# First mixer: the rotation's powers computed directly behind the angles

## The reference

```python
h = rmsnorm(x); z = h @ w_in                      # (tokens, 1536): u of group A, u and v of group B
dt = exp(log_dt); mag = exp(lam_re * dt)
ab = mag * (cos(lam_im * dt) + 1j * sin(lam_im * dt))
bb = (ab - 1) / lam * B                           # B: 32 groups x 64 states x 16 inputs
h[t] = ab * h[t-1] + bb @ u[t]                    # complex, one state vector per group
yA = glu(gelu(Re(C h) + D * u))
yB = gelu(uB) * (tril(W_s) @ layernorm(gelu(vB)) + b)
x = x + [rmsnorm(yA), rmsnorm(yB)] @ w_out
x = x + FFN(rmsnorm(x))                           # layer 0: dense SwiGLU, layer 1: top-2-of-8 experts
```

## Time and profile before

| | us |
|---|---|
| median of three executions | 865.59 |
| the profiled execution | 866.52 |
| its span, first to last instruction | 864.7 |
| PE busy | 820.4 (95%) |
| DVE busy | 564.0 (65%) |
| ACT busy | 403.0 (47%) |
| POOL busy | 243.9 (28%) |

### The profile page before, as it was taken

How to read it: one execution, slowest core, us unless ns; L and a number is a source line. 1 busy time by engine, 2 the same in 40 slices (tenths; PEclk the granted TensorE clock), 3 DMA queues, 4 the chain that set the end, 5 groups by cost and what they waited for, 6 DMA issues and landing times.

```text
span 864.7 us, 13823 instructions
## 1 busy us (share of the span) xinstructions
PE 820.4 (95%) x5086; PEld 639.5 (74%) x5086; DVE 564.0 (65%) x997; ACT 403.0 (47%) x606; POOL 243.9 (28%) x206
## 2 busy tenths in 40 slices
PE   8997999999989999999989998999999998999994
PEld 7576779999989999858767877887877442865332
DVE  7999667566966567566952699899855230964115
ACT  6787354455324432278341396686734020850102
POOL 3794124121334462425111001504214000132002
PEclk9998999999999999999999899999999999999998
DMA  9600913755556531560220298998999999999993
GB/s 295 199 2 4 343 31 109 250 165 142 158 158 163 166 116 50 144 205 1 100 107 1 102 420 342 346 306 273 378 358 381 423 420 420 422 413 422 420 413 117
DMA packets 89330, 200.75 MB, mean 232 GB/s; under 512 B 26144, under 2 KB 47888, under 8 KB 89264
## 3 DMA queue, kind: packets, MB, share of 16 engines
q1 hardware_dynamic: 88464, 198.86, 62.9%
q10 hardware_dynamic: 576, 0.59, 0.2%
q0 software_dynamic: 224, 0.43, 0.2%
HBM read 198.25 MB, written 1.61 MB: 231 GB/s over the span
## 4 chain that ended last, share of the span: by engine, by line
PE 60%; DVE 13%; SPq 9%; POOL 6%; ACT 4%; DMA 4%; issue 4%; DVEq 0%; POOLq 0%; ACTq 0%
SPq L766 8%; PE ps L1322 7%; PE ps L1321 7%; PE ps L1323 6%; PE ps L1510 5%; PE ps L1638 3%; PE ps L1622 3%; PE ps L1623 3%; PE ps L1625 3%; PE ps L1765 2%; PE ps L1766 2%; PE ps L1769 2%; DMA wraw_d<-in_moe_w_gate 2%; PE ps L1400 2%; PE ps L1336 2%
## 5 line engine op out<-in xcount | busy, mean ns | idle before, releaser
L1321 PE MATMUL ps<-Md,split_u 128*128 128x288 f32 (+2 forms) x304 | 89.6, 295 | 0.0
L1323 PE MATMUL ps<-Md,split_u 128*128 128x288 f32 (+2 forms) x304 | 89.1, 293 | 0.0
L1822 DVE TENSOR_TENSOR xb<-xb,ps 128x288 f32<-128x288 f32 x80 | 33.3, 450 | 64.9 <-PE ps L1510 26.6
L826 POOL TENSOR_TENSOR wrnd_g<-wraw_g,wrnd_g 128x1024 fp32r<-128x1024 f32 (+1 forms) x6 | 17.1, 2848 | 179.3 <-ACT wrnd_g L1014 179.3
L1322 PE MATMUL ps<-hbr,split_u 128*128 128x288 f32 (+1 forms) x192 | 57.1, 297 | 0.0
L1822 DVE TENSOR_TENSOR wrnd_g<-wraw_g,wrnd_g 128x1376 fp32r<-128x1376 f32 (+2 forms) x31 | 48.7, 1587 | 12.9 <-ACT wrnd_g L1014 12.7
L1323 PEld LDWEIGHTS ps<-Md,split_u 128*128 128x128 f32 (+2 forms) x304 | 56.9, 187 | 0.0
L1321 PEld LDWEIGHTS ps<-Md,split_u 128*128 128x128 f32 (+2 forms) x304 | 56.8, 187 | 0.1
L1822 DVE TENSOR_TENSOR wrnd_d<-wraw_d,wrnd_d 128x1376 fp32r<-128x1376 f32 (+2 forms) x20 | 34.0, 1730 | 34.9 <-ACT wrnd_d L1014 34.9
L1008 ACT ACTIVATE split_u<-raw 128x1024 fp32r<-128x1024 f32 (+2 forms) x38 | 39.6, 1048 | 36.1 <-PE ps L1323 36.1
L1822 DVE TENSOR_TENSOR wrnd_u<-wraw_u,wrnd_u 128x1376 fp32r<-128x1376 f32 (+2 forms) x34 | 56.3, 1686 | 0.0
(11 more groups left out here) (464 smaller groups left out, 2250.1 us busy)
## 6 DMA issues: line engine op xcount, KB each, us to landing
wraw_g<-in_moe_w_gate SPq DMA_DIRECT2D x31, 688.0 KB, 10.1
wraw_u<-in_moe_w_up SPq DMA_DIRECT2D x29, 688.0 KB, 17.1
wraw_d<-in_moe_w_gate SPq DMA_DIRECT2D x22, 688.0 KB, 9.3
wraw_g<-in_moe_w_down SPq DMA_DIRECT2D x28, 512.0 KB, 15.2
wraw_u<-in_moe_w_down SPq DMA_DIRECT2D x28, 512.0 KB, 13.3
raw<-in_ffn_w_gate SPq DMA_DIRECT2D x20, 512.0 KB, 4.5
raw<-in_ffn_w_up SPq DMA_DIRECT2D x20, 512.0 KB, 4.1
raw<-in_ffn_w_down SPq DMA_DIRECT2D x20, 512.0 KB, 4.3
```

Of the source, the lines that this page charges most:

```text
L1321: pe.matmul(out, w_hi, x_hi, start=start, stop=False)
L1323: return pe.matmul(out, w_lo, x_hi, start=False, stop=stop)
L1822: return dve.tensor_tensor(o, a, b, op)
```

## The change

For layer 0 the call of `rotation_powers(sv)`, five squarings of five instructions each on 128x16 values, moves from behind B's powers to directly behind the angles. The instructions are the same.

```diff
@@ -2001,6 +2001,7 @@
                     root_inverse()
                     scaled_u()
                 else:
+                    rotation_powers(sv)
                     dve.wait_ge(prep_in, 16)
                 tight1, tight2 = [t[:, 0:NP * GH].rearrange("p (n f) -> p n f", n=NP) for t in (lt, sg)]
                 for s in range(0 if l else CH):
@@ -2023,7 +2024,6 @@
                         dve.wait_ge(const_in, 32)
                         dve.tensor_reduce(sel, ident.rearrange("p (g i) -> p i g", i=NSAMP), AX.X, ALU.add).then_inc(sel_ready, 1)
                 if l == 0:
-                    rotation_powers(sv)
                     magnitudes()
                     scaled_u()
                 link(dve.memset(stat, 1.0))
```

## The result

The changed kernel takes 871.59 us (median of six executions, 870.9 to 874.47) against 865.85 for the kernel before in the same comparison: ratio 1.0076, 95% interval 1.0058 to 1.0094. That is 5.7 us more, where +3.9 was forecast. The profiled execution took 870.96 us with a span of 869.0.

What follows compares the result with a forecast made beforehand. TensorE (95% busy) was taken as the bound nearly everywhere, waiting 4.36 us at line 1418. Contention of 12.0 less 8.1 starts y 3.9 us late, carried to the end: 869.5 us, range 862 to 873 (forecast alone 867 to 872).

Steps and rivals of the forecast that it cites:

- The move itself: Squarings go to 12.84 us on VectorE, B's powers begin at 16.52, GpSimd's n = 2 at 13.63, n = 8 at about 17.2.
- What stands beside GpSimd: VectorE's two-input instructions on B's powers held up by GpSimd's table: sum 12.5 us, taken as 12.0; end 41.2 instead of 26.3.
- the 0.5: Taken off the 12.5 us of contention on B's powers, because links on either side overlap some of the holds.
- the reciprocal's 1.7 us: Extra on B's powers if VectorE's reciprocal excludes GpSimd's n = 16 too; taken as 0; chance 0.15 together with rival 2.
- The way over ScalarE: Restacking u at 43.8 us, 11.4 late; transposes' copies 59.05; line 1392's q = 2 65.2; line 1129 until 84.35.
- the 1.4 us from the end of line 1141's copies to `k_ready`: Last step on ScalarE's chain before y: 1.4 us more, giving `k_ready` at 92.0.
- The 1.8 us for line 1418: TensorE's line 1418, 3.67 us at half clock before, given 1.8 us, on the way to TensorE being ready at 91.8.
- rival 2: TensorE's clock falls where work is awaited, low between 60 and 72 us; chance 0.15 together with the reciprocal's 1.7 us.
- Rival 1: VectorE keeps its pace on B's powers, contention near 0: y at 81.1, -7.1 us, 858.5; chance 0.17 with what lies between.
- the rule that y's shift is the contention less 8.1: Lateness from contention on B's powers enters y's start one for one; the shift is zero at 8.1 us.

Runs made afterwards that it cites:

- e5: e3 with four more GpSimd tensor_tensor of 128x512 and a short memset ahead of them, beside B's last powers: 865.12 us, ratio 0.9996 to the kernel before.
- e6: e3 with five GpSimd memsets of 128x1024 and a short memset ahead of them, beside B's last powers: 862.71 us, ratio 0.9964 to the kernel before.
- e2: The changed kernel, but GpSimd waits for B's last power before the doubling n = 16: 865.15 us, ratio 0.9986 to the kernel before.
- e9: The changed kernel with the edits of e3 and e8 together: 860.4 us, ratio 0.9942 to the kernel before.
- e8: The changed kernel, but SP issues the first layer's w_out loads only after y's third quarter: one execution, 869.64 us.
- e4: The changed kernel with 40 matmuls whose result nobody reads ahead of TensorE's wait for `vp_ready`: 871.25 us, ratio 1.0071 to the kernel before.
- e7: The changed kernel, but two of five squarings run behind `scaled_u`; GpSimd waits for B's last power before line 886, n = 16, n = 32: 863.33 us, ratio 0.9975.
- e3: The changed kernel, but GpSimd waits for B's last power before line 886, behind n = 16: 862.44 us, ratio 0.9952 to the kernel before.
- e1: The changed kernel, but GpSimd waits for B's last power before the doubling n = 2: 870.12 us, ratio 1.0041 to the kernel before.

## Why the prediction was right, and where it was short

The direction, the mechanism and the way to the end were as forecast; the size was short by a third (+3.9 for +5.7).

- *The move itself*: n = 2 at 13.62 (13.63), B's powers from 16.51 (16.52), n = 8 at 17.29 (17.2). As said.
- *What stands beside GpSimd*: the list gave 12.5 us, and 0.5 was taken off for overlap. B's powers ended at 41.7 instead of 41.2, so 12.5 was right and the 0.5 was not there. It was right by its terms too: 2.4 us beside n = 8 and 16 (2.5 listed), 2.1 beside line 886 (2.1), 5.3 beside n = 32 (5.4), 2.7 beside the masks (2.5). The rows show each instruction held until the other engine's has ended, e5 and e6 show what it takes for that, and the reciprocal's 1.7 us did not come.
- *The way over ScalarE*: restacking 44.30 (43.8), copies 59.52 (59.05), line 1392's second half at about 65.9 (65.2), line 1129 until 85.0 (84.35), line 1141's copies until 91.28 (90.6). The steps were right to 0.2 us, over the 0.5 carried along.
- *The term that was mis-sized*: the 1.4 us from the end of line 1141's copies to `k_ready`. In the kernel before it is 1.43, with 1.26 for GpSimd's line 940. In the change it is 2.13, as line 940 takes 1.95: it has come to stand beside a scan of VectorE, which reads two inputs, and ends 1.06 us behind the scan's end (92.35), about the time of another GpSimd instruction of this width (1.09 for line 853). y starts 0.05 us behind line 940's end; the 0.70 us in its bracket are TensorE's idle time from 92.75 on. The same holds in e2 to e9, where line 940 ends 1.05 to 1.06 us behind the scan each time. So the exclusion that the prediction priced on B's powers came once more, the other way round, on the last step before y, which the prediction took over from the kernel before. The profile's chain of waits runs through it. With the 0.7 carried along from above this makes the 1.36 between 92.1 and 93.46.
```profile
86.27 1.26 POOL L940 TENSOR_TENSOR M<-M,D 128x512 f32<-128x512 f32 x1 [12.63 <-ACT M L1141]
```
```profile
91.15 1.20 DVE L2149 TENSOR_TENSOR_SCAN G<-U,G 128x512 f32<-128x512 f32 x1
91.46 1.95 POOL L940 TENSOR_TENSOR M<-M,D 128x512 f32<-128x512 f32 x1 [12.63 <-ACT M L1141]
```
- *Not seen at all*: the pause inside y, 1.14 us for 0.27. It makes the other 0.9. e8 ties it to the loads, e4 to the place in TensorE's stream as well; its cause stays open. All in all +3.9 + 1.36 + 0.9 = +6.1, beside +5.7 by the medians and +6.6 by the ratio.
- *TensorE's clock*: the forecast adds nothing for it, and the low clock after the wait at line 1364 (0.50 from 46 to 50 us) delayed nothing that y waits for. In part this is luck: it stretched line 1367 until 58.9 (9.33 us, against 7.13 at a granted clock of 1.00 in e4), so that TensorE was not idle between 57 and 65, but ran without a gap from 47.72 to 92.75. In e4, with a granted clock of 1.00 from 43 to 54, it waited 2.56 us there and the clock fell on awaited work (0.57 from 60 to 64). The 1.8 us for line 1418 are half of its 3.67, for a clock of 0.50 that the kernel before was granted there (80 to 82 us); no run shows the 1.8, the line took 2.02 us at a granted clock of 1.00 (86 to 90). But rival 2, a clock that falls where the work is awaited, is real: it came in e2, e4 and e7, behind waits of 1.1 to 2.6 us near the transposes and states; y started 1.2 us later than in the change in e4, and 2.5 and 4.2 us later than expected in e2 and e7.
- *Rival 1* fell in the profile, and e5 against e6 leaves nothing of it. What it promised, -7.1 us, was half there to be had: e3 gives -4.2 with a contention of 2.4 us (31.6 less 29.2). By the rule that y's shift is the contention less 8.1, y comes 0.7 to 0.8 us late in all three versions that it covers (the change, e3, e5), which is line 940's hold; with it the break-even is at 7.4 us, an estimate from these three, as no run lies on it.

## What to carry to other kernels

An engine that idles is not free to start early: ask what its instructions read, and which instructions of another engine then stand beside them. Here the idle 14 us of GpSimd were what let B's powers run at full pace (0.42 us for an instruction that took up to 2.57 in the change); an early start paid clearly only once the long instructions were held behind the last of B's powers, with one wait on a semaphore that was there already (e3). And what a stall at the end of a chain gives back has to be weighed against the chain that takes its place, step by step: a step's length, taken over from the kernel before, can change with what the other engine does beside it, as the 0.7 us of line 940 did.

The stall itself was in large part of this kind. C's powers, on GpSimd, last 18.4 us in the kernel before (54.64 to 73.02), beside VectorE's rotations, and 12.0 in the change (48.38 to 60.34), where VectorE has no two-input instruction from 51.2 on (it idles 7.30 us and then runs the statistics). At that pace they would have been ready at 66.6 (an estimate from these two), ahead of the end of ScalarE's centring at 67.2. No version tried to keep VectorE off them.

## What the runs showed of the hardware

- VectorE's tensor_tensor with both inputs in SBUF and GpSimd's tensor_tensor exclude each other instruction by instruction: 0.42 us recorded became 2.57 beside one GpSimd instruction on a single partition (line 886). Shown is this for 64 partitions x 256 values (0.68 us beside n = 8 in the kernel before, at 32.83) and more; the 16-wide squarings beside n = 2 and 4 show no stretching (25 in 3.64 us). It holds the other way too: GpSimd's line 940 took 1.95 us instead of 1.26 beside a TENSOR_TENSOR_SCAN. GpSimd's memsets beside two-input instructions (e6, 0.42 us each), VectorE's reciprocal (1.95 us either way), and instructions that read one input from PSUM (three in 1.18 us with and without a doubling beside them) were free of it. Four GpSimd instructions that read cost B's powers 3.1 us (e5), five that only write 0.05 (e6).
- One input is not always free. In e1 the first doubling of n = 2 starts beside VectorE's copy of 1024 values and takes 0.69 us, against 0.25 in the kernel before. And in the kernel before a tensor_scalar of 16 values (line 1912) takes 2.24 us, until GpSimd's memset of line 878 has ended; the tensor_scalars of line 1916 on, with GpSimd idle, take 0.17.
- Waits of TensorE of 1.38, 2.56 and 1.06 us were followed by a granted clock of 0.50 from 58 to 62 us in e2, 0.52 from 60 to 62 in e4 and 0.50 from 58 to 62 in e7; waits of 1.24 and 2.62 us at the transposes in e3 and e5 were not (1.00 from 50 to 70). In e2 and e7 the wait stood between the two halves of the states, in e4 at the transposes as in e3 and e5. What tells them apart stays open.
- TensorE pauses up to 1.17 us in the middle of y, with nothing awaited, at one place in its stream while large loads run; not when they are held (e8, e9), and not when forty more matmuls stand ahead in the stream (e4). What causes the pause no run shows.
